# The second matrix product of both feed-forward layers in seven half-size products, with block sums written by adding DMAs

## The reference

```python
def conv_ffn(x, hist, g, w_up, cw, cb, w_down):
    h = rms_norm(x, g)
    u = jnp.einsum('btd,df->btf', h, w_up)
    ext = jnp.concatenate([hist.astype(u.dtype), u], axis=1)
    T = u.shape[1]
    c = cb + sum(cw[j] * ext[:, j: j + T] for j in range(CONV_W))
    a, b = jnp.split(c, 2, axis=-1)
    out = jnp.einsum('btf,fd->btd', jax.nn.silu(a) * b, w_down)
    return out, ext[:, -(CONV_W - 1):]
```

## Time and profile before

| | us |
|---|---|
| median of 3 runs | 2339.62 (2336.34 to 2340.19) |
| profiled execution, its own time | 2340.53 |
| its span, first to last instruction | 2338.7 |
| PE busy in it | 2251.4 (96%) |
| up-projections, in the chain that ended last | 36.5% (L1200) |
| down-projections, in the same chain | 19.5% (L1289) |
| mean granted TensorE clock | 0.977 |

### The profile page before, as it was taken

How to read it: one execution, slowest core, us unless ns; L and a number is a source line. 1 busy time by engine, 2 the same in 40 slices (tenths; PEclk the granted TensorE clock), 3 DMA queues, 4 the chain that set the end, 5 groups by cost and what they waited for, 6 DMA issues and landing times.

```text
span 2338.7 us, 46142 instructions
## 1 busy us (share of the span) xinstructions
PE 2251.4 (96%) x17427; PEld 2194.6 (94%) x17427; DVE 1544.3 (66%) x2393; ACT 974.2 (42%) x1806; POOL 241.0 (10%) x337
## 2 busy tenths in 40 slices
PE   7899999999999999999999998888999999999999
PEld 7899999998999999999999886578999999989999
DVE  4778888887455566374462776467788888764444
ACT  4554455455344433132231543225544444553333
POOL 1000000000011044152341220021000000000000
PEclk8999999999999999999999998899999999999999
DMA  5222222224654622222223786531222222266555
GB/s 187 73 64 81 73 74 78 81 83 164 237 172 142 215 81 78 96 83 93 79 75 105 234 281 180 169 119 64 73 81 77 76 81 81 68 219 211 192 181 163
DMA packets 204887, 290.39 MB, mean 124 GB/s; under 512 B 14343, under 2 KB 145719, under 8 KB 204498
## 3 DMA queue, kind: packets, MB, share of 16 engines
q1 hardware_dynamic: 199970, 284.00, 37.3%
q10 hardware_dynamic: 4792, 4.68, 0.6%
HBM read 226.64 MB, written 69.72 MB: 127 GB/s over the span
## 4 chain that ended last, share of the span: by engine, by line
PE 88%; DVE 5%; DMA 3%; ACT 2%; issue 1%; SPq 1%; POOL 0%; ACTq 0%; DVEq 0%; POOLq 0%
PE ps L1200 36%; PE ps L1289 20%; PE ps L1885 6%; PE ps L1883 6%; PE ps L1884 6%; PE ps L394 3%; PE ps L2121 2%; PE ps L2094 1%; DMA kvt<-kvs 1%; PE ps L2105 1%; PE ps L2061 1%; PE ps L2133 1%; PE ps L826 1%; PE ps L452 1%; PE ps L1880 1%
## 5 line engine op out<-in xcount | busy, mean ns | idle before, releaser
L1200 PE MATMUL ps<-hT,w 128*128 128x258 f32 x2752 | 461.1, 284 | 3.7 <-DVE w L1042 2.3
L1200 PEld LDWEIGHTS ps<-hT,w 128*128 128x128 f32 x2752 | 387.2, 191 | 4.6 <-DVE w L1042 2.7
L1289 PE MATMUL ps<-gdh,whl 128*128 128x384 f32 (+1 forms) x1472 | 351.1, 319 | 0.7 <-DVE x L1499 0.7
L1200 PE MATMUL ps<-lT,w 128*128 128x258 f32 x1376 | 277.5, 283 | 0.0
L1289 PEld LDWEIGHTS ps<-gdh,whl 128*128 128x128 f32 x1472 | 255.4, 188 | 1.7 <-DVE x L1499 1.3
L1289 PE MATMUL ps<-gdl,whl 128*128 128x384 f32 (+1 forms) x736 | 234.1, 318 | 0.0
L1200 PE MATMUL ps<-hB,w 128*128 128x258 f32 x1344 | 229.6, 282 | 4.4 <-DVE ub L1399 4.4
L1200 PEld LDWEIGHTS ps<-lT,w 128*128 128x128 f32 x1376 | 214.6, 191 | 0.0
L1200 PEld LDWEIGHTS ps<-hB,w 128*128 128x128 f32 x1344 | 191.0, 189 | 4.8 <-DVE ub L1399 4.8
L1151 ACT ACTIVATE w<-sq 128x1024 fp32r<-128x1024 f32 x84 | 88.8, 1057 | 174.6 <-PE ps L1200 169.4
L1479 DVE TENSOR_TENSOR whl<-stage,whl 128x1024 fp32r<-128x1024 f32 x62 | 75.9, 1224 | 109.9 <-ACT whl L1488 109.9
(11 more groups left out here) (346 smaller groups left out, 5413.2 us busy)
## 6 DMA issues: line engine op xcount, KB each, us to landing
stage<-in_w_down SPq DMA_DIRECT2D x100, 512.0 KB, 3.6
stage<-in_w_up SPq DMA_DIRECT2D x176, 256.0 KB, 3.2
gs<-cb SPq DMA_DIRECT2D x44, 516.0 KB, 2.7
graw<-gs SPq DMA_DIRECT2D x80, 192.0 KB, 3.7
rb<-in_w_down SPq DMA_DIRECT2D x30, 512.0 KB, 3.5
stage<-in_w_kv SPq DMA_DIRECT2D x24, 512.0 KB, 4.0
kvs<-kn SPq DMA_DIRECT2D x48, 256.0 KB, 2.0
xsp<-x SPq DMA_DIRECT2D x16, 516.0 KB, 2.7
```

The costliest lines, as they stand in the source:

```text
L1200: mm = pe.matmul(ps[:, bank + c, 0:HB], w, m[:, c * HB:(c + 1) * HB], start=(first and i == 0), stop=(i == len(parts) - 1), skip_group_che ...
L1289: mm = pe.matmul(ps[:, d, 0:n], wt_, m, start=(f == 0 and i == 0), stop=(f == NF - 1 and i == 2))
```

## The change

The down-projection becomes the same seven-product scheme. w_down and the activations are cut in halves along the 2816 features (11 tiles each), along the 1024 outputs (4 tiles each) and along the 1032 columns (516 each, run as 2 x 258). Each of seven products, in the order P1, P6, P7, P4, P5, P3, P2, runs over 11 tiles p and 4 output tiles d with 3 x 2 matmuls, so 24 matmuls of 258 columns per step and 77 steps per layer. PSUM keeps accumulating from one product to the next where the scheme's partial results allow it (a fresh start only in products 0, 4 and 6), and after each product DVE adds the four pairs of banks to, or subtracts them from, one quadrant of x.

The scheme needs sums of blocks: four of the weights (`wsum`) and four of the activations (`tsum`). They are made in DRAM. POOL issues DMAs that copy and DMAs that add to what they write; each waits for those before it on which it depends. For a tile e of the first 11, that is 11 DMAs of about 256 KB in 6 rounds (a round ends with a wait for all issued so far), for a tile of the last 11, 5 DMAs in 4 rounds. POOL starts on tile e's activation part when `f_kept` says that tile e is stored. PE's second product (P6) is the first that reads the sums, and SP's load for its tile p waits until the sums of tile 11 + p are finished. A negated half of every tile is needed too: ACT writes it (`gn`), and SP stores it as `gneg`, behind the store of `gs`.

```diff
+        PRODUCTS = ("P1", "P6", "P7", "P4", "P5", "P3", "P2")
+        NP = NF // 2
+        NSTEPS = 7 * NP
+        FRESH = (0, 4, 6)
+        TARGETS = ((0, 1), (0, 0), (1, 0), (1, 1), (1, 0), (0, 0), (0, 1))
...
+        def sp_down(sp, L, S, n):
+            i, p = n // NP, n % NP
...
+            if n >= 4:
+                sp.wait_ge(f_dl, S.dl + 2 * n - 6)
...
+            if i == 1:
+                sp.wait_ge(sums_in, summed(L, NP + p))
+            sp.dma_start(dwr[slot], wsrc).then_inc(f_wd_in[n % 4], 16)
...
+            sp.dma_start(dxr[slot], xsrc).then_inc(f_wd_in[n % 4], 16)
...
             def keep(f):
                 sp.wait_ge(f_prod, f + (S.prod + 1))
                 sp.dma_start(gs[L, bass.ds(f, 1)].rearrange("o p n -> p (o n)"), cb[:, :]).then_inc(f_kept, 16)
...
+                sp.wait_ge(f_silu_ng, 2 * f + (S.silu + 2))
+                sp.dma_start(gneg[L, bass.ds(f, 1)].rearrange("o p n -> p (o n)"), gn[:, :]).then_inc(f_kept, 16)
...
+                for j, (w, m) in enumerate(three(dwh[slot][:, cols], dwl[slot][:, cols], dxh[slot], dxl[slot])):
+                    for c in range(2):
+                        mm = pe.matmul(ps[:, 2 * d + c, 0:HB], w, m[:, c * HB:(c + 1) * HB],
+                                       start=(i in FRESH and p == 0 and j == 0), stop=(last and j == 2), skip_group_check=True)
...
+        def act_down(act, S, n):
+            i, slot = n // NP, slot_of(n)
+            act.wait_ge(f_wd_in[n % 4], S.wd_in[n % 4] + 32 * (n // 4) + 32)
+            act.wait_ge(*((f_pr, product_done(S, NF - 1, "P5" if n < 4 else "P4")) if n < 8 else step_done(S, n - 4)))
+            nc.scalar.activation(dwh[slot], dwr[slot], ACT.Copy).then_inc(f_dh, 1)
+            nc.scalar.activation(dxh[slot], dxr[slot], ACT.Copy, scale=-1.0 if i == 1 else 1.0).then_inc(f_dh, 1)
...
+        def pool_sums(q, L, S):
...
+                if e < NP:
+                    q.dma_start(s1, a1[:, AL]).then_inc(sums_in, 16)
+                    q.dma_start(s3, a1[:, AH]).then_inc(sums_in, 16)
+                    done += 32
+                    q.wait_ge(sums_in, done)
+                    q.dma_start(s1, a2[:, AL], accum_op=ALU.add).then_inc(sums_in, 16)
+                    q.dma_start(s3, a1[:, AL], accum_op=ALU.add).then_inc(sums_in, 16)
+                    done += 32
+                    q.wait_ge(sums_in, done)
+                    q.dma_start(s2, s1).then_inc(sums_in, 16)
...
+                    q.wait_ge(f_kept, S.kept + 32 * (e + 1))
+                    q.dma_start(t2, t1).then_inc(sums_in, 16)
+                    q.dma_start(t3, half(gs[L, e], 0), accum_op=ALU.add, max_dma_last_dim=4 * N).then_inc(sums_in, 16)
...
+        def adds_after(S, i):
+
+            return NP * (i + 1) + (1 if paired(S.L, i) else 2)
...
+            def negated(f, h):
+                act.wait_ge(f_prod, f + (S.prod + 1))
+                nc.scalar.activation(gn[:, :], half(cb, h), ACT.Copy, scale=-1.0).then_inc(f_silu_ng, 1)
...
+            negated(f, 1)
             act_conv_tails(act, L, S, TAILS[NF, 0])
```

More of the change, by code:

```diff
@@ L887, in up_src, with paired, steps_before, step_done @@
             return w[:, KH * part:KH * part + KH, bass.ds(f * P + half_ * F, P)]
[L889 to L910, removed]
+        def paired(L, i):
+            return i == 6 or (L == 1 and i in (3, 5))
+        def steps_before(L, i):
+            return sum(NP - 2 if paired(L, j) else NP - 1 for j in range(i))
+        def step_done(S, n):
+            i, p = n // NP, n % NP
+            if p < NP - 2 or (p == NP - 2 and not paired(S.L, i)):
+                return (f_dn, S.dn + steps_before(S.L, i) + p + 1)
+            return (f_fin, S.fin + KH * (i + 1))
+        def slot_of(n):
+            return 4 + n if n < 4 else n % 4
+        def quadrant(t, i, d):
+            D1, h = TARGETS[i]
+            return half(t[:, KH * D1 + d, :], h)
         def product_done(S, f, name):
@@ new lines, in step, with last_two @@
+                for d in range(KH):
+                    if p == 0:
+                        free(i, d)
+                    mm = one(n, d, p == NP - 1)
+                    if p == NP - 1:
+                        mm.then_inc(f_fin, 1)
+                if p < NP - 1:
+                    mm.then_inc(f_dn, 1)
+            def last_two(i):
+                n = NP * i + NP - 2
+                ready(n)
+                ready(n + 1)
+                for d in range(KH):
+                    one(n, d, False)
+                    one(n + 1, d, True).then_inc(f_fin, 1)
@@ L1351, in build @@
+            for d in range(3):
+                one(1, d, False)
+            pe_conv_tails(pe, S, TAILS[NF, 0])
+            free(0, 3)
+            one(0, 3, False).then_inc(f_dn, 1)
+            one(1, 3, False).then_inc(f_dn, 1)
+            for i in range(7):
+                for p in range(2 if i == 0 else 0, NP - 2 if paired(L, i) else NP):
+                    step(NP * i + p)
+                if paired(L, i):
+                    last_two(i)
         TAILS = {(NF - 3, 0): (0, 1), (NF - 3, 1): (2, 3), (NF - 2, 0): (6, 7), (NF - 2, 1): (8, 9), (NF - 1, 0): (4,),
@@ new lines, in added, with dve_split_quad, pool_quads @@
+        def added(j):
+            return j + 1 - (1 if j < 4 else 2)
+        def dve_split_quad(v, S, Sx, i, d):
+            v.wait_ge(split_hi, Sx.hi + KH * QUADS[i] + d + 1)
+            nc.vector.tensor_tensor(quadrant(xl, i, d), quadrant(x, i, d), quadrant(xh, i, d).bitcast(F32),
+                                    ALU.subtract).then_inc(split_lo, 1)
+        def pool_quads(g, Sx):
+            for i in (3, 4, 5, 6):
+                for d in range(KH):
+                    j, h = KH * QUADS[i] + d, TARGETS[i][1]
+                    if j in (0, 4):
+                        continue
+                    g.wait_ge(split_sq, Sx.sq + j + 1)
+                    if added(j - 1):
+                        g.wait_ge(split_acc, Sx.acc + added(j - 1))
+                    nc.gpsimd.tensor_tensor(half(acc, h), half(acc, h), half(sq[:, d % 2, 0:N], h), ALU.add).then_inc(split_acc, 1)
@@ new lines, in pe_result @@
+        def pe_result(pe, r, d):
+            pe.wait_ge(f_xa, ffn[1].xa + KH * (3, 5, 6)[r] + d + 1)
+            for c, parts in enumerate(RESULTS[r]):
+                for D1, tiles in parts:
+                    for k, t in enumerate(tiles):
+                        mm = pe.transpose(ps[:, 2 * d + c, k * P:(k + 1) * P], x[:, KH * D1 + d, t * P:(t + 1) * P], ident[:, :])
+            if r != 1:
+                mm = pe.transpose(ps[0:NS, 2 * d + r // 2, 3 * P:4 * P], x[:, (KH if r == 0 else 0) + d, T:N], ident[:, :])
+            mm.then_inc(wo_y_pe, 1)
```

557 lines of the change are left out of this document (296 added, 261 removed).

## The result

The changed kernel takes 2508.1 us (median of 4 runs, 2504.5 to 2511.4), the kernel before on the same chip 2338.5. The ratio is 1.0724, 95% interval 1.0710 to 1.0737: slower by 7.2%, where 2299 us was predicted and the range ended at 2440.

The account below looks back on a forecast made before the run. The prediction took PE to bound the kernel. Its terms, -51.8 - 1.9 + 2.3 + 8.8 + 0.5 - 0.8 + 2.3, summed to -40.6 us, giving 2299 us against the median, with a range of 2286 to 2440.

Parts of the forecast that it names:

- The adding DMAs: POOL's rounds making the block sums: expected to fit a 462 us budget per layer, 35 to 87 us inside, cost 0.
- L, a round of one DMA: Time of a POOL round with one DMA: taken as 3.2 to 3.7 us, where 4.04 us was allowed.
- A further DMA in a round: Each DMA beyond the first in a POOL round: taken as 0.69 us, 262 KB at 388 GB/s.
- The sums come late: Rival: P6's loads wait on POOL's rounds and PE behind them, from L = 4.04; 2395 or 2499 us; chance 0.27.
- Matmuls removed: Both down-projections: 77 steps of 24 shorter matmuls per layer, 221.9 us for 247.8; -51.8 us over both layers.
- Feeding and product ends: Down-projection: ACT and DVE stay under the 2.88 us step, cost 0; product ends -1.9 in layer 0, +2.3 in layer 1.
- Between the projections: Handover from up- to down-projection: tails' copies wait behind the negation, 4.4 us per layer, +8.8 in all.
- Layer 0's end and the launch's end: Shorter last-step parts before layer 0's projection, -0.8 us; about 7.2 us after the launch's last matmul, +2.3.
- The sum without the DMA term: All predicted terms added, with the adding DMAs at cost 0: -40.6 us.
- POOL locked out by DVE: Rival: POOL's DMAs wait for DVE instructions in the up-projection; 2323 us, with whole instructions 2521; chance 0.05.
- Starved weight loads: Rival: up-projection weight loads land after more than 8 us, then 40 us per us; 9 us gives 2340; chance 0.04.
- The page's estimate: The Trainium skill's formula for a GpSimd-issued DMA, giving L = 2.6 us for POOL's rounds, inside the budget.

Follow-up runs that it names:

- experiment 4: Changed kernel with every adding DMA made a plain copy of the same rows, so no sums are made; rounds, waits and gate stay: 2318.1 us, ratio 0.9916.
- Experiment 6: Changed kernel with one add left out of each round that holds two, rounds and waits kept: 2421.8 us, ratio 1.0363.
- experiment 1: Changed kernel without POOL's sum DMAs and SP's wait on them; products read plain pieces of the same size: 2302.8 us, ratio 0.9864.
- experiment 7: Changed kernel with the DMAs of two neighbouring tiles in each round, nothing left out: 2304.7 us, ratio 0.9864; in a second comparison 2307.9 us, 0.9872.
- experiment 2: Changed kernel with all of POOL's DMAs issued, but nobody waits for or reads the sums; readers take plain pieces: 2336.7 us, ratio 0.9998.

## Why the prediction was wrong, point by point

**The step that failed** is the last term, "The adding DMAs". Its frame was right: a chain of rounds from tile 0's storing to PE's step 21, with a budget of 462 us, and beyond it every us paid in both layers. The chain ran in layer 0 from 162.41 (the second tile's first round) to 720.6, 558 us, 96 over the budget. What was wrong is its length, by two sizes:

- **L, a round of one DMA.** Taken: 3.2 to 3.7. Measured: 3.92 and 4.70 in the first-half tiles, 4.47, 4.07 and 4.69 in the others, weighted by their number 4.4, at the load of these stretches. By the prediction's formula that is 104 x 4.4 + 42.1 = 500 us, 38 over. The value came from the weight loads of the stage before the change. They are plain loads at a DMA share of 0.24, and with the change they themselves take 4.2 us at 0.70. The rival noticed that 0.45 would be added to the share, yet the chosen value didn't move. And the half us for reading the target was too little: an add is 0.8 us above a copy in one tile (4.70 against 3.92), and experiment 4 puts the price of adding, with the shorter rows of a part of the adds, at 190 us of the whole.
- **A further DMA in a round.** Taken: 0.69 us, from a peak of 388 GB/s (262 KB at that rate are 0.68). The 61 further DMAs of ten first-half and eleven second-half tiles cost the rest of the chain, 58 us over the 42.1 allowed, 1.6 us each: 1.0 to 1.2 for a copy, 2.2 to 2.5 for an add. This term had no range in the prediction. By the prediction's own figures the chain should have lasted 375 to 427 us; of the 131 to 183 it lasted longer, L made 73 to 125 and this term 58. L's miss alone would have put the chain 38 us over the budget; this term's alone 23 over at L = 3.7, and not over at 3.2. Experiment 6 shows it by itself: 86 us, where 0.69 would give 30.

**How much it cost.** The changed kernel's span is 207 us above that of experiment 1. PE's waits on `gdl` are 171.3 of it, those on x at a product end 3.5, 0.8 more at the tails, and 29.7 are PE's busy time (2228.3 against 2198.6 for the same 17944 matmuls). The mean granted clock was 0.71 from 575 to 720, and the 459 matmuls there took 66.7 us where 0.1201 each would be 55; the earlier trace rows had shown a clock of 0.50 behind a pause of 3.29 us. The prediction priced the lateness without this. Per layer it is 15 us on 84 us of pauses.

**The rival "The sums come late"** is what happened. It gave 2499 us at L = 5, and the chain of 558 us is that of L = 5.0 in its formula. It had 0.27, and the range ended at L = 4.7. The unknown cost's upper end, 6.3, was in the text and was left out of the range. Its sign came, waits in P6 that a DMA of the sums ends; but they don't grow with p: each of the last six is about one tile's chain (18 to 20 us) less one step at the lowered clock.

**Matmuls removed**: right. -51.8 predicted; PE's busy time falls by 52.8 in experiment 1 and by 50.8 in 7.

**Feeding and product ends**: right in layer 0. One piece of 1716 matmuls stands there without a wait. In layer 1 PE waits three times for x in all, 3.2 us (0.4 before): 2.8 where 2.3 was expected.

**Between the projections**: right. +8.8; the wait for the tails' copy grows from 6.6 to 16.0 us, +9.4.

**Layer 0's end and the launch's end**: the projection's start falls from 5.8 to 5.3 us, -0.5 for -0.8, though it is 5.6 in the changed kernel and in 7. At the launch's end 9.0 us follow the last matmul's row at 2288.00 instead of 7.2, +4.1 for +2.3.

**The sum without the DMA term** was -40.6 us. By medians of the same comparison experiment 1 is 34.4 below the kernel before, and experiment 7, with all sums made and read, 32.4. So the sum promised some 6 to 8 us too much. The profiled executions flatter it: their spans are 41.7 and 38.7 below, but 1's was the fastest of its four, which spread from 2298.8 to 2309.5. In which term the missing 6 us lie no run shows.

**POOL locked out by DVE**: not what happened. A copy takes POOL 0.52 us to issue and an add 0.8, both at 240.74 and 243.88, where DVE is busy 84% of the time, and at 695.37 and 698.48, where it mostly idles. And the rounds of experiment 2 are longest where DVE is busy 53% of the time and the DMA share is 0.93. The Trainium skill ("SBUF — State Buffer", Who interferes with whom) has two-input work of DVE leave GpSimd's writing alone. The trace agrees with that: from 150 to 500 DVE ran two-input work only. For the one-input modes that the page names as the ones that lock, this stretch has no case.

**Starved weight loads**: not what happened. They land in 4.2 us for 3.2, and PE is busy 350.00 of 350 us.

**The page's estimate.** The Trainium skill ("DMA: Bandwidth & Descriptors", Anatomy of one DMA) gives 2.0 us + bytes / 436 GB/s for a DMA issued by GpSimd, an estimate of 2.6 us for 256 KB. The trace comes near that only for a lone copy with PE standing. The chain has its flight and that of an add:

```profile
695.37 2.83 DMA tsum<-tsum
...
716.64 3.98 DMA tsum<-gneg
```

With the 0.2 to 0.3 us until POOL's next issue the copy's round is 3.1 us. An add, or any DMA beside the up-projection, is far above the estimate (3.9 to 4.7 a round), and the measurement decides. The estimate made the forecast look safe from a third side.

## What to carry to other kernels

Price a chain of dependent DMAs by rounds and by what a round holds, at the load that the change itself creates, and an adding DMA higher than a copy; a landing time from the lighter stage before is a lower end, not the middle. Where such a chain has to meet a date, make its rounds fewer and fuller: twice the DMAs in each took the same bytes from 720.6 to about 617 us. A range must hold the far end of a cost that is multiplied by a hundred, and an engine's own later work stands behind the DMAs in its queue, also where nobody reads what they bring.

## What the runs showed of the hardware that was not expected

- An adding DMA is much dearer than a copy of the same bytes. In the up-projection a lone add of 256 KB takes 4.7 us from POOL's issue to its next one, a lone copy 3.9; a second add in the round 2.2 to 2.5 more, a second copy 1.1. With PE nearly idle it is still 4.1 to 4.4 against 3.1. The same bytes need half as many packets again (31328 against 20768, in part by the shorter rows of the adds of `gneg`). POOL issues an add in 0.8 us and a copy in 0.5.
- The length of a round goes with the load. A lone add takes 4.1 to 4.4 us at a DMA share of 0.51, 4.7 at 0.70 and 5.7 to 5.8 at 0.93; a lone copy 3.2, 3.9 and 4.65 (at 0.70 the DMAs are those of the weights, at the two others those of the activations).
- Halving a DMA's bytes and rows takes a fifth to a quarter off a round, and doubling the DMAs per round makes it less than twice as long. What each DMA of this size pays beyond its bytes is, by an estimate from these two sizes, about 2.8 us for a lone add (3.75 at 128 KB, 4.70 at 256 KB, drawn on to none) and 2.2 for a lone copy (3.06 and 3.92).
- 176 more DMAs per layer, at a DMA share of 0.70 instead of 0.24, cost PE nothing in layer 0's up-projection from 150 to 500 us.
